# The scan stage of a hybrid SSD and attention layer: PE's output products behind the first projection pieces of a slot, and DVE's masks, finish, weighted rows and mix in a new order

## The reference, cut to what matters

```python
def ssd_scan(x, dt, a_log, b_in, c_in, init_state):        # 32 heads in 8 groups, chunks of 128
    A = -jnp.exp(a_log)
    xdt = x * dt[..., None]
    a_cs = jnp.cumsum(dt * A, axis=2)
    seg = a_cs[:, :, :, None, :] - a_cs[:, :, None, :, :]
    decay_in = jnp.exp(jnp.where(lower, seg, -jnp.inf))
    scores = jnp.einsum('bclhn,bcshn->bclsh', Ch, Bh)
    y_diag = jnp.einsum('bclsh,bcshp->bclhp', scores * decay_in, xdt)
    chunk_states = jnp.einsum('bclhn,bclh,bclhp->bchpn', Bh, decay_to_end, xdt)
    def step(s, inp):
        st, dc = inp
        return s * dc[:, :, None, None] + st, s
    final, prev = lax.scan(step, init_state, (chunk_states, chunk_decay))
    y_off = jnp.einsum('bclhn,bchpn,bclh->bclhp', Ch, prev, jnp.exp(a_cs))
    return y_diag + y_off, final
...
y = y_f + fl(y_b) + lp['d_skip'][:, None] * xs
y = rmsnorm(y.reshape(bsz, t, SSD_D_INNER) * jax.nn.silu(z), lp['ssd_norm_w'])
merged = jax.nn.sigmoid(g_a) * y_a + jax.nn.sigmoid(g_b) * y_b2
```

## Time and profile before

| | |
|---|---|
| median of three runs | 2761.56 us (2760.55 to 2767.19) |
| the profiled execution | 2762.55 us, of which 2760.8 us are its span |
| granted TensorE clock over the span | 0.958 |
| PE busy | 2520.0 us (91%) |
| DVE busy | 2125.2 us (77%) |
| ACT busy | 1139.0 us (41%) |
| POOL busy | 866.1 us (31%) |

### The profile page before, as it was taken

How to read it: one execution, slowest core, us unless ns; L and a number is a source line. 1 busy time by engine, 2 the same in 40 slices (tenths; PEclk the granted TensorE clock), 3 DMA queues, 4 the chain that set the end, 5 groups by cost and what they waited for, 6 DMA issues and landing times. The chain is left out here.

```text
span 2760.8 us, 39138 instructions
## 1 busy us (share of the span) xinstructions
PE 2520.0 (91%) x14998; PEld 2205.5 (80%) x14998; DVE 2125.2 (77%) x3681; ACT 1139.0 (41%) x1946; POOL 866.1 (31%) x623
## 2 busy tenths in 40 slices
PE   5989999988999996988799887999999999999996
PEld 4868888787778775988788586888888888888885
DVE  3657777713788875433699795999999999999998
ACT  4235556524565654322443385232333323333332
POOL 0000000003667663110044284344334433434431
PEclk9999999998999997999899998999999999999998
DMA  6531122223224222533222268999999999999995
GB/s 242 220 113 51 66 100 83 81 95 119 98 77 134 88 68 84 180 109 112 95 78 64 94 201 313 417 419 409 417 416 416 418 413 414 418 414 417 416 406 231
DMA packets 166266, 621.50 MB, mean 225 GB/s; under 512 B 14880, under 2 KB 83264, under 8 KB 105664
## 3 DMA queue, kind: packets, MB, share of 16 engines
q1 hardware_dynamic: 124608, 340.03, 33.2%
q0 software_dynamic: 36864, 268.45, 23.6%
q10 hardware_dynamic: 4608, 10.52, 1.2%
HBM read 559.39 MB, written 59.56 MB: 224 GB/s over the span
## 5 line engine op out<-in xcount | busy, mean ns | idle before, releaser
L2324 POOL DMA_INDIRECT p_uv<-in_uv_rows,merged x256 | 396.3, 1548 | 624.8 <-DVE merged L2491 564.1
L2491 DVE SCALAR_TENSOR_TENSOR merged<-p_uv,p_sw,merged 128x1024 f32<-128x1024 f32 x256 | 330.7, 1292 | 7.1
L2474 DVE CUSTOM_DVE_ANT_0 p_uv<-p_uv,merged 128x1024 f32<-128x1024 f32 x256 | 310.2, 1228 | 17.5 <-DMA p_uv<-in_uv_rows,merged 17.5
L2344 PE MATMUL p_pa<-h2D,w_hi 128*128 128x384 f32 x896 | 318.8, 356 | 4.5 <-DVE w_lo L2445 2.3
L2346 PE MATMUL p_pa<-h2D,w_lo 128*128 128x384 f32 x896 | 302.7, 338 | 0.0
L2345 PE MATMUL p_pa<-h2D,w_hi 128*128 128x384 f32 x896 | 302.6, 338 | 0.0
L2388 ACT ACTIVATE w_hi<-w_raw 128x2048 fp32r<-128x2048 f32 x110 | 210.4, 1913 | 177.6 <-DMA w_raw<-in_w_stream 104.9
L2359 PE MATMUL p_py<-w_hi,p_wh 128*128 128x512 f32 x672 | 266.9, 397 | 14.2 <-DVE w_lo L2445 14.0
L2445 DVE TENSOR_TENSOR w_lo<-w_raw,w_hi 128x2048 fp32r<-128x2048 f32 x110 | 251.7, 2288 | 23.7 <-ACT w_hi L2388 23.7
L2361 PE MATMUL p_py<-w_hi,p_wl 128*128 128x512 f32 x672 | 266.0, 396 | 0.0
L2360 PE MATMUL p_py<-w_lo,p_wh 128*128 128x512 f32 x672 | 265.9, 396 | 0.0
(11 more groups left out here) (386 smaller groups left out, 6202.8 us busy)
## 6 DMA issues: line engine op xcount, KB each, us to landing
w_raw<-in_w_stream SPq DMA_DIRECT2D x174, 1024.0 KB
g_pairs<-e_st SPq DMA_DIRECT2D x5, 4096.0 KB, 16.4
p_g<-g_pairs SPq DMA_DIRECT2D x64, 320.0 KB
t_ada<-in_w_ada SPq DMA_DIRECT2D x16, 1024.0 KB, 10.2
xc_dram<-c_xc SPq DMA_DIRECT2D x8, 1284.0 KB, 5.4
p_ve<-in_v_early SPq DMA_DIRECT2D x8, 1024.0 KB, 13.9
r_ur<-in_u_early ACTq DMA_DIRECT2D x14, 512.0 KB, 3.7
s_xx<-xc_dram SPq DMA_DIRECT2D x8, 642.0 KB, 6.3
```

What stands on the lines that cost most here:

```text
L2324: nc.gpsimd.indirect_dma_start(uv[:, k % RING, :], None, K.uv_rows, bass.IndirectOffsetOnAxis(K.sidx[:, t, c:c + 1], 0)).then_inc(K.gather ...
L2344: nc.tensor.matmul(ps_a[m][:, :], wh[:, k, cols], K.h2D[0][:, k, :], start=k == 0, stop=False)
L2474: nc.vector.tensor_tensor_reduce(uv[:, b, 0:D], uv[:, b, 0:D], K.hrow[:, t, :], 1.0, 0.0, ALU.mult, ALU.add, sa[:, at:at + 1]).then_inc(do ...
L2491: nc.vector.scalar_tensor_tensor(ys[:, t, :], uv[:, b, D:2 * D], sw[:, at:at + 1], ys[:, t, :], ALU.mult, ALU.add).then_inc(v_done, 1)
```

## The change

In each slot, PE's `outputs(f)` goes from the slot's start to behind the first part of the pieces, ahead of `transposes(a)`. On DVE, `masks(b)` goes ahead of `finish(f)`, and `mix(b)` goes behind `weighted(a)`. No instruction is added or removed, and ACT, POOL and SP keep their order.

```diff
             for q in range(SLOTQ):
                 a, b, f = ssd_steps(q)
                 todo = pieces_of(q)
-                if f is not None:
-                    outputs(f)
                 if 1 <= q <= STEPS:
                     states(q - 1)
                 if b is not None:
                     between(b)
                 for u, i in todo[:split_point(todo)]:
                     piece(u, i)
+                if f is not None:
+                    outputs(f)
                 if a is not None:
                     transposes(a)
                 for u, i in todo[split_point(todo):]:
                     piece(u, i)
...
             for q in range(SLOTQ + 1):
                 a, b, f = ssd_steps(q)
+                if b is not None:
+                    masks(b)
                 if f is not None:
                     finish(f)
-                if b is not None:
-                    masks(b)
-                    mix(b)
                 if a is not None:
                     weighted(a)
+                if b is not None:
+                    mix(b)
                 for u in last_pieces(q - 1):
                     S.lo(dve, U_ZG + u + 2, u % 2)
```

## The result

| | median | runs | ratio to before |
|---|---|---|---|
| before | 2760.55 us | 5 | |
| after | 2773.99 us | 5 | 1.0054 (1.004 to 1.0068) |

The kernel became 13 us slower, where 28 us faster was forecast. The profiled execution has a span of 2775.7 us, 14.9 more than before.

The account below looks back on a forecast made before the run. PE was taken as the bound, though not a clean one: 34.9 us it lacks, less 7 (new waits), 2 (ACT) and 2 (clock), gives 24, with the tail 28 us saved; forecast 2734 us, range 2720 to 2757.

Parts of the forecast that it names:

- The step that failed: PE's s_pst: weighted rows would be ready earlier than now, so its 4.7 us of waits would go.
- PE's loop from y to y: What PE needs from one s_py end to the next: 4.0 us plus the one or two pieces between.
- DVE's loop through M: From y through finish, weighted rows and mix to M and s_py: 6.6 to 8.9 us.
- Ten places that decide: Places with one piece between two PE outputs, out of 36: 7 us of new waits together.
- The mix becomes quiet: On DVE, POOL nearly through when the mix begins: L1419 and L1422 near 0.7 us, the 1.00 wait for s_A gone.
- the rule of the Trainium skill: POOL contends with two-SBUF-input DVE instructions: three finish operations slowed by 1.1 us wherever the masks come just ahead.
- A wait that is new in kind: DVE's weighted rows, now ahead of the mix, wait for ACT's token-row copy: four slots, half a us each, 2 us.
- The clock: PE's granted clock of 0.97 cost 11 us from 680 to 1057 us; 2 us of loss was to stay.
- The tail: From 1057 to 1085 us, three output rounds lose the masks and s_A wait from their path: 4 us saved.
- The slower rival: M waits return mid-slot at ten short places and the clock falls at each: 13 us slower, 2775 us; chance 0.08.

Follow-up runs that it names:

- e4: The changed kernel with the weighted rows put ahead of the finish on DVE; 2755.50 us, ratio 0.9990.
- e3: The changed kernel with the single piece of a one-piece slot put behind the transposes instead of ahead of the outputs; 2748.46 us, ratio 0.9967.
- e8: The changed kernel with transposes ahead of outputs, weighted rows ahead of finish, and the low half behind the next masks; 2746.73 us, ratio 0.9957.
- control kernel: The kernel before the change, with only the single pieces of one-piece slots put behind the transposes; 2748.22 us, ratio 0.9961.
- e12: e10 with ACT's high half of a weight unit moved from the slot's end to behind the next slot's token rows; 2735.41 us, ratio 0.9916.
- e10: e8 with the single pieces of one-piece slots also put behind the outputs; 2743.52 us, ratio 0.9939.

## Why the prediction was wrong, point by point

- **The step that failed** is the sentence "the weighted rows for s_pst are ready earlier than now, so the 4.7 us go". The weighted rows did move ahead of the mix. But what they need, the transposes, moved behind the outputs, and the finish, which needs these same outputs, went in between on DVE. From s_py to the weighted rows there are 1.0 to 3.7 us of finish and 0.75 to 1.6 of weighting, and PE has only the transposes (0.5) to fill it with where the slot has no second piece. I had summed PE's loop from y to y and DVE's loop through M, and had not asked for the third consumer, s_pst. Measured: 33.8 us where 0 stood, 31.3 of it at the ten places. Without the finish ahead of the weighted rows the loss is gone (e4, ratio 0.9990).
- **Ten places that decide**: right in number and place, wrong in what is waited for there. I priced 7 us for M and masks; M cost nothing and the masks nothing.
- **The mix becomes quiet**: right. L1419 and L1422 run at 0.69 us and the waits for s_A are gone. The finish pays some of it back, as weighed by the rule of the Trainium skill (GPSIMD Engine Reference, Key points): L1439, never over 0.43 us before, now goes up to 1.13. It did not decide: at six of the ten places the finish took its plain 2.5 us or less, and the wait was still 1.95 to 3.24 us. At the other four it took 3.1 to 3.7, which is 3.6 us in all of the 31.3.
- **A wait that is new in kind** (weighted behind ACT): 2 us forecast, at most 0.25 us at any of the ten places in after, where the finish covered it. It came up at the longest wait of e3 (2.92 us), and in e4 and e8, once the weighted rows stood first.
- **The clock**: the 11 us lost before are about right (375.26 - 364.84 = 10.4 by the control kernel, which has PE's outputs at the same place and a clock of 1.00). I let 9 of them come back. Instead the loss about doubled. e12 has the outputs behind the first piece, as after does, and needs 357.9 us at full clock; against it after lost 22.5 us. So the clock took some 12 us more, and the new order gave some 7 us of busy time back (364.8 - 357.9), a term that was not in my sum at all. The 12 and the 7 are an estimate, since e12 differs from after in five edits; the net 5.1 us is measured. The mean clock says about the same: 3% of 403 us before, 6% of 418 us after.
- **The tail**: 4 us forecast, 4.5 found, but not by the path I priced alone. The wait for M fell from 10.8 to 0.6 us, and new waits came up, of 5.7 us at s_pT and 2.1 for the finish.
- **The slower rival** gave 2775 us, and 2774 was measured, but for another reason: it had M waiting in mid-slot. The number was a coincidence of the ten places and about 3 us each. It was given 0.08 since I asked only what speaks for M being late.

Put with measured sizes, my own sum would have been: idle 37.8 - 27.5, busy time + 5.1, tail - 4.5, that is 10.9 us slower. Another 1.5 us of the measured difference lie ahead of the first gate piece, and 2.4 outside the stage. Open is what part of e10's 15.3 us for the masks is due to ACT and what to POOL beside the finish, and why the order of e12 needs 7 us less busy time than the old one at the same clock.

## What to carry to other kernels

When work is moved on an engine that others wait for, list every consumer of every moved instruction and of those it is moved behind, and sum each path from its last input, at the shortest slot: here two of three loops got shorter and the third decided. Put the fill (here a piece) between an operation and the next one that needs what another engine makes of it, in each slot and not only in those with two pieces. And a wait costs more than its length if the clock falls behind it (here 1.7 us more behind one of 1.85), so two short waits can be cheaper than one long one of the same sum. The control kernel shows it: 10.4 us of busy time less at nearly the same idle time.

## What the runs showed of the hardware that was not expected

- The same PE work took 357.9, 364.8, 375.3 or 380.4 us of busy time (e12, control, before, after), at a mean clock of 1.00, 1.00, 0.97 and 0.94, with 17.5, 26.0, 27.5 and 37.8 us of idle time. Between the second and the third the idle time is nearly the same; what differs is how it is dealt out. Between the first and the second the clock is the same and only the order of the work differs, which makes 7 us; what in it does was not tested. In after, each of the waits of 2.23 us and more at the ten places was followed by s_pst at 1.7 to 2.1 us instead of 1.08; waits of 1.27 us and less were not. In the control kernel two waits of 2.5 us at the transposes did not lower the clock noticeably. So length alone doesn't tell it, and what does was not tested.
- A DVE operation with both inputs in SBUF beside POOL can take three times as long (L1439 1.27 us against 0.42), not only twice as L1422 did (1.41 against 0.69). The Trainium skill (GPSIMD Engine Reference, Key points) names this contention; its size is from these rows.
